# Seven-product feed-forward blocks: the remainder of the fourth weight slot moves from GpSimd to VectorE, and one corner is summed by matmuls onto a bank that ScalarE has filled

## The chip, the cores and the metric

The program runs on one core of a Trainium2 chip. The time is that of the device for one launch, in microseconds (us); lower is better.

## What is computed

The reference is an encoder of two layers on 512 tokens of width 1024, in float32. Each layer normalises its input, projects it, runs a latent attention and a state-space branch, mixes them, and then does a feed-forward (SwiGLU) block:

```
h   = x + W_o(...)
out = h + (silu(n @ w_gate) * (n @ w_up)) @ w_down      # n = RMSNorm(h)
```

`w_gate` and `w_up` are 1024 x 2816, `w_down` is 2816 x 1024. Only this block of the last layer (l = 1) is touched by the change.

## The kernel before, in words

Every float32 operand of a matmul is held as a high part (rounded to fp32r) and a low part (the remainder), and a product is three matmuls: high by high, high by low, low by high. ScalarE writes the high parts (`wh`), another engine subtracts them from the original to get the low parts (`wl`).

The last layer's gate and up projections are done by a scheme with seven products in place of eight. A step is one pair block q (0 to 21, even q is gate, odd q is up): two blocks of 128 output rows, by the two halves of the tokens (256 each), over the two halves of the inner dimension. Its weights come in two slabs of 512 KB (`pair_slab(q)` and the next). From them VectorE forms four sums (`sums_first`: two, `sums_last`: two). Four slots of `wh` and `wl` hold what the products read: slot 0 is the first slab as it is (P1 and P2), slot 1 the first two sums (P5, P6), slot 2 the last two (P3, P7), slot 3 one half of the second slab (P4). Each product is 12 matmuls of 256 columns.

The blocks come in three parts (`PARTS`): q = 0 to 7, 8 to 15 and 16 to 21. After each part its hidden rows go through the down projection (`down_steps`), whose weights use the same slots and stages.

TensorE's order in a block q is P2, P1, P5, P4 of block q-1 (called `corner`), P6, P3, P7. P6 adds onto P1's bank, P3 onto P5's, and P7 onto the bank of P6. PSUM banks: P2 in 2 + q%2, P1, P6, P7 and P4 in 4 + q%2, P5 and P3 in 6 + q%2.

The first corner of the output is P2 minus P1: ScalarE copies P1 to `part_sums` (`first_copied`), and VectorE subtracts it from P2 (`first_sum`, line 2065). The other three come from `corner` and `two`, `five` on ScalarE (copies) and from `other_sums` on VectorE (lines 2070 and 2073).

The loads have an order of their own. Four stages hold slabs, so pair q + 2 goes where pair q was. SyncE issues the loads in order, and for each it waits until the stage is free:

```
def freed_by_pair(q, i):
    sp.wait_ge(s34_ready, q + 1)
    sp.wait_ge(op_lo[0], q + 1)
    if i:
        sp.wait_ge(op_lo[3], q + 1)
```

`s34_ready` comes from `sums_last(q)`, `op_lo[0]` from VectorE's `low(0, q)`, `op_lo[3]` from the subtraction for slot 3, which in this kernel GpSimd does (line 724). On the other side `sums_first(q)` waits until both slabs of pair q have landed.

On each engine the work of the stage is a list in program order. ScalarE, in block q: `high(2, q)`, `first_copied(q)`, `high(0, q+1)`, `five(q)`, `corner(q-1)`, `high(3, q)`, `two(q)`, `high(1, q+1)`, `finished(q-1)`. VectorE: `other_sums(q-1)`, `low(2, q)`, `sums_first(q+1)`, `first_sum(q)`, `low(0, q+1)`, `sums_last(q+1)`, `scaled(q-1)`, `low(1, q+1)`, and in even blocks `rest(q-1)`.

Of the kernel before, what the change touches and what calls it, by code (L numbers as in the profile page):

```python
# [62 lines left out]
            "P7": (2, 1, X7), "P4": (3, 0, X4)}  # L63


def part_of(q):
    return next(h for h, (first, count) in enumerate(PARTS) if q < 2 * (first + count))

# [9 lines left out]
def pair_slab(q):  # L78
    return 2 * q + KT * part_of(q)
# [11 lines left out]
DONE = {}  # L91
for h in range(len(PARTS)):
    for q in range(first_of(h), last_of(h) + 1):
        for name in ("P2", "P1", "P5", "P4", "P6", "P3", "P7"):
            if name != "P4":
                DONE[q, name] = len(DONE) + 1
            elif q > first_of(h):
                DONE[q - 1, name] = len(DONE) + 1
    DONE[last_of(h), "P4"] = len(DONE) + 1
# [24 lines left out]
def build(nc, xT, stream, gcols, gqk, grows, dskip, params, cmat, rope, ident_in, out):  # L124
    with ExitStack() as ctx:
# [497 lines left out]
        def _(pool):  # L623
# [94 lines left out]
                for n in range(S_UP + 3, SLABS if l + 1 < DEPTH else S_FFN):  # L718
                    remainder(SLABS * l + n)

            for q in range(FB):
                s = fast_slot(3)
                pool.wait_ge(op_hi[3], q + 1)
                pool.tensor_tensor(wl[:, s, 0:QT], fast_stage(pair_slab(q) + 1)[:, QT:2 * QT],  # L724
                                   wh[:, s, 0:QT].bitcast(F32), ALU.subtract).then_inc(op_lo[3], 1)

        @block.scalar
        def _(act):
# [508 lines left out]
            def high(i, q):  # L1237
                if q == first_of(part_of(q)):
                    h = part_of(q)
                    if h:  # L1240
                        act.wait_ge(slab_done, RING + plain(h - 1, KT - RING + i) + 1)
                    else:
                        act.wait_ge(slab_done, RING + LAST - RING + i + 1)
                else:
                    act.wait_ge(prod_done, DONE[q - 1, ("P1", "P6", "P7", "P4")[i]])
                o = wh[:, fast_slot(i), :]
                if i == 0:
                    fast_loaded(pair_slab(q))
                    copy(o, fast_stage(pair_slab(q))).then_inc(op_hi[0], 1)
                elif i == 1:  # L1250
                    act.wait_ge(s12_ready, q + 1)
                    copy(o, wsum[:, 0:2, :].rearrange("p i c -> p (i c)")).then_inc(op_hi[1], 1)
                elif i == 2:
                    act.wait_ge(s34_ready, q + 1)
                    copy(o, wsum[:, 2:4, :].rearrange("p i c -> p (i c)")).then_inc(op_hi[2], 1)
                else:
                    fast_loaded(pair_slab(q) + 1)
                    copy(o[:, 0:QT], fast_stage(pair_slab(q) + 1)[:, QT:2 * QT]).then_inc(op_hi[3], 1)

            def down_high(h, m):  # L1260
                z, w = down_slab(h, m), 2 * PARTS[h][1] * P
                fast_loaded(z)
                if m < RING:
                    act.wait_ge(prod_done, DONE[last_of(h), ("P1", "P6", "P7", "P4")[m]])
                else:
                    act.wait_ge(slab_done, RING + plain(h, m - RING) + 1)
                copy(wh[:, fast_slot(m), 0:w], fast_stage(z)[:, 0:w]).then_inc(wh_ready, 1)
# [36 lines left out]
            def first_copied(q):  # L1304
                act.wait_ge(prod_done, DONE[q, "P1"])
                if q >= 2:
                    act.wait_ge(c11_done, q - 1)
                copy(part_sums[:, q % 2, 0, :], ps[:, 4 + q % 2, 0:HTOK]).then_inc(p_copied, 1)

            def five(q):  # L1310
                act.wait_ge(prod_done, DONE[q, "P5"])
# [25 lines left out]
            for h in range(len(PARTS)):  # L1337
                first, last = first_of(h), last_of(h)
                for q in range(first, last + 1):
                    high(2, q)  # L1340
                    first_copied(q)
                    if q < last:
                        high(0, q + 1)
                    else:
                        down_high(h, 0)
                    five(q)
                    if q > first:
                        corner(q - 1)
                    high(3, q)
                    two(q)  # L1350
                    if q == 0:
                        act.wait_ge(stat_ready, 2 * l + 2)
                        act.activation(rscol[:], ps[:, 0, 0:TT], ACT.Sqrt, bias=eps[:], scale=1.0 / D_MODEL).then_inc(rms_ready, 1)
                    if q == 1:
                        act.wait_ge(stat_ready, 2 * l + 3)
                        copy(RS[:], ps[:, 0, :]).then_inc(rms_ready, 1)
                    if q < last:
                        high(1, q + 1)
                    else:
                        down_high(h, 1)  # L1360
                    if q > first:
                        finished(q - 1)
                down_high(h, 2)
                corner(last)
                down_high(h, 3)
                finished(last)
                for m in range(KT):
                    if m < RING:
                        down_high(h, m + RING)
                    elif h + 1 < len(PARTS) and m < RING + 2:  # L1370
                        high(m - RING, last + 1)

        @block.vector
        def _(dve):
# [619 lines left out]
            def low(i, q):  # L1994
# [3 lines left out]
                dve.wait_ge(op_hi[i], q + 1)  # L1998
                tt(wl[:, s, :], source, wh[:, s, :].bitcast(F32), SUB).then_inc(op_lo[i], 1)  # L1999

            def down_low(h, m):
                s, w = fast_slot(m), 2 * PARTS[h][1] * P
                dve.wait_ge(wh_ready, plain(h, m) + 1 - RAW)
                tt(wl[:, s, 0:w], fast_stage(down_slab(h, m))[:, 0:w], wh[:, s, 0:w].bitcast(F32), SUB).then_inc(wl_ready, 1)
# [86 lines left out]
            for h in range(len(PARTS)):  # L2091
                first, last = first_of(h), last_of(h)
                for q in range(first, last + 1):
                    if q > first:
                        other_sums(q - 1)
                    low(2, q)
                    if q < last:
                        sums_first(q + 1)
                    first_sum(q)
                    if q < last:  # L2100
                        low(0, q + 1)
                        sums_last(q + 1)
                    else:
                        down_low(h, 0)
                    if q == 1:
                        dve.wait_ge(rms_ready, 2 * l + 3)
                    if q > first:
                        scaled(q - 1)
                    if q < last:
                        low(1, q + 1)  # L2110
                    else:
                        down_low(h, 1)
                    if q == 0:
                        dve.wait_ge(rms_ready, 2 * l + 2)
                        dve.reciprocal(rscol[:], rscol[:]).then_inc(rs_ready, 1)
                    if q > first and q % 2 == 0:
                        rest(q - 1)
# [25 lines left out]
        def _(pe):  # L2143
# [442 lines left out]
            def steps(q, name, ks):  # L2586
                i, half, o = PRODUCTS[name]
                bank = {"P2": 2, "P5": 6, "P3": 6}.get(name, 4) + q % 2
                s = fast_slot(i)
                for k in ks:  # L2590
                    if q == 0:
                        pe.wait_ge(xt_ready if o in (X4, X5, X6, X7) else xb_ready, k + 1)
                    at = slice(half * QT + k * P, half * QT + (k + 1) * P)
                    last = products(ps[:, bank, 0:HTOK], (wh[:, s, at], wl[:, s, at]), (XH[:, o, k, :], xl_of(o)[:, k, :]),
                                    k == 0 and name in ("P2", "P1", "P5"),
                                    k == 3, name not in ("P2", "P1", "P5"))
                return last

            def opening(q, name):
# [26 lines left out]
            for h in range(len(PARTS)):  # L2626
                first, last = first_of(h), last_of(h)
                count = 2 * PARTS[h][1]
                for q in range(first, last + 1):
                    if q == 0:  # L2630
                        for name in ("P1", "P5", "P2"):
                            if name == "P2":
                                pe.wait_ge(xm_ready, KT * l + 3 + KT)
                            opening(q, name)
                            steps(q, name, range(3))
                        for name in ("P2", "P1", "P5"):
                            steps(q, name, (3,)).then_inc(prod_done, 1)
                    else:
                        for name in ("P2", "P1", "P5"):
                            opening(q, name)  # L2640
                            steps(q, name, range(4)).then_inc(prod_done, 1)
                    if q == 1:
# [4 lines left out]
                    if q > first:  # L2647
                        corner(q - 1)
                    pe.wait_ge(p_copied, q + 1)
                    steps(q, "P6", range(4)).then_inc(prod_done, 1)  # L2650
                    if q == 0:
                        pe.wait_ge(x2_ready, KT * l + KT + 2)
# [115 lines left out]
```

## Time and profile before

| | |
|---|---|
| median of 3 runs | 1523.31 us (1523.0 to 1526.86) |
| the profiled execution, its own time | 1524.58 us |
| its span | 1522.4 us |
| TensorE busy | 1486.8 us, 98% |
| VectorE busy | 1099.5 us, 72% |
| ScalarE busy | 670.6 us, 44% |
| GpSimd busy | 462.0 us, 30% |
| stage of the change | from 1168 us to the end of the span |

The profile is one execution. PE is TensorE, PEld its weight loads, DVE is VectorE, ACT ScalarE, POOL GpSimd and SPq the queue of SyncE, which issues the loads. A row of a timeline gives start, duration, engine, line, operation, what is written and read, and in brackets the idle time before it and what ended that. L730 is a helper with which ScalarE does all its copies, L1999 is `low` for three slots, L2146 to L2148 are the three matmuls of a product.

### The profile page before, as it was taken

Reading aid. Unit: us, or ns where it says so; the run is one execution under the profiler, and the core shown is the slowest. Engines: PE = TensorE matmul, PEld = TensorE weight load, DVE = VectorE, ACT = ScalarE, POOL = GpSimd, SP = SyncE. Lnnn points to the kernel's source line nnn. Section 1 sums busy time; section 2 is a strip of 40 time slices with the busy share of each in tenths; the row PEclk is TensorE's granted clock in tenths of the full one; section 3 lists DMA queues with packets and bytes.
Section 4 is the critical chain, followed back from the end, with each engine's and each line's share of the span. In section 5 each row is a group of like instructions: output and inputs, shape, how many; then the busy total and the mean of one; then the engine's idle time right before and its main releaser. Section 6 shows DMA issues by size and latency. Waiting matters only on the chain.

```text
span 1522.4 us, 23041 instructions
## 1 busy us (share of the span) xinstructions
PE 1486.8 (98%) x8954; PEld 1221.0 (80%) x8954; DVE 1099.5 (72%) x1469; ACT 670.6 (44%) x1146; POOL 462.0 (30%) x254
## 2 busy tenths in 40 slices
PE   8999998999999999999999999999999999999998
PEld 3555897878878878887888888887787998998997
DVE  5999888768448997568432782586888995896794
ACT  4563258852452222232332413587435652453361
POOL 0000053544444454443544323444542120110010
PEclk9999999999999999999999999999999999999999
DMA  6568720142333244443437642102331333234223
GB/s 248 163 195 294 296 84 1 43 124 83 97 113 97 77 167 158 145 140 112 163 106 276 214 153 89 56 1 70 111 103 65 111 97 126 84 99 137 70 92 116
DMA packets 73499, 189.51 MB, mean 124 GB/s; under 512 B 23600, under 2 KB 32176, under 8 KB 69296
## 3 DMA queue, kind: packets, MB, share of 16 engines
q1 hardware_dynamic: 41952, 145.18, 28.3%
q10 hardware_dynamic: 31440, 42.87, 8.7%
q8 instruction: 71, 1.16, 0.3%
q14 instruction: 36, 0.29, 0.1%
HBM read 155.52 MB, written 32.51 MB: 124 GB/s over the span
## 4 chain that ended last, share of the span: by engine, by line
PE 67%; DVE 17%; DVEq 5%; ACT 4%; issue 3%; DMA 1%; POOLq 1%; POOL 1%; SPq 0%; ACTq 0%
PE ps L2146 20%; PE ps L2148 20%; PE ps L2147 20%; PE ps L2295 2%; DVE wl L1999 2%; DVE work L1382 1%; ACT prob L1148 1%; PE ps L2201 1%; PE ps L2272 1%; DVEq L1562 1%; DVEq L1509 1%; PE ps L2240 1%; DVE wsum L1990 1%; PE ps L2286 1%; PE ps L2459 1%
## 5 line engine op out<-in xcount | busy, mean ns | idle before, releaser
L632 POOL TENSOR_TENSOR wl<-stage,wh 128x1024 fp32r<-128x1024 f32 x138 | 356.7, 2591 | 645.2 <-ACT wh L730 456.2
L730 ACT ACTIVATE wh<-stage 128x1024 fp32r<-128x1024 f32 (+2 forms) x178 | 181.0, 1023 | 221.9 <-PE ps L2148 103.4
L2146 PE MATMUL ps<-XH,wh 128*128 128x256 f32 x616 | 174.8, 284 | 3.7 <-DVE wl L1999 2.8
L2148 PE MATMUL ps<-XH,wl 128*128 128x256 f32 x616 | 173.8, 282 | 0.0
L2147 PE MATMUL ps<-XLr,wh 128*128 128x256 f32 x528 | 148.5, 281 | 0.0
L2146 PE MATMUL ps<-xg2h,wh 128*128 128x512 f32 x352 | 140.3, 399 | 0.0
L2148 PE MATMUL ps<-xg2h,wl 128*128 128x512 f32 x352 | 139.2, 396 | 0.0
L2147 PE MATMUL ps<-xg2l,wh 128*128 128x512 f32 x352 | 139.2, 396 | 0.0
L2146 PEld LDWEIGHTS ps<-XH,wh 128*128 128x128 f32 x616 | 116.8, 190 | 5.2 <-DVE wl L1999 3.2
L2148 PEld LDWEIGHTS ps<-XH,wl 128*128 128x128 f32 x616 | 116.8, 190 | 0.0
L2201 PE MATMUL ps<-X,slabs 128*128 128x512 f32 x224 | 100.7, 604 | 7.2 <-DMA X<-in_xT 5.8
L2147 PEld LDWEIGHTS ps<-XLr,wh 128*128 128x128 f32 x528 | 99.8, 189 | 0.2
L2201 PEld LDWEIGHTS ps<-X,slabs 128*128 128x128 f32 x224 | 42.2, 193 | 58.9 <-issue 46.5
L2146 PE MATMUL ps<-xgh,wh 128*128 128x512 f32 x208 | 84.4, 406 | 0.0
L2148 PE MATMUL ps<-xgh,wl 128*128 128x512 f32 x208 | 82.3, 396 | 0.0
L2147 PE MATMUL ps<-xgl,wh 128*128 128x512 f32 x208 | 82.3, 396 | 0.0
L2146 PEld LDWEIGHTS ps<-xg2h,wh 128*128 128x128 f32 x352 | 66.1, 188 | 16.3 <-issue 0.6
L2148 PEld LDWEIGHTS ps<-xg2h,wl 128*128 128x128 f32 x352 | 66.1, 188 | 16.0
L2147 PEld LDWEIGHTS ps<-xg2l,wh 128*128 128x128 f32 x352 | 66.2, 188 | 15.9 <-issue 0.2
L724 POOL TENSOR_TENSOR wl<-stage_more,wh 128x512 fp32r<-128x512 f32 x11 | 17.8, 1616 | 198.7 <-ACT wh L730 198.7
L2146 PE MATMUL ps<-hidh,wh 128*128 128x512 f32 x176 | 70.2, 399 | 3.2 <-DVE X L1968 1.7
L2146 PE MATMUL ps<-hid1h,wh 128*128 128x512 f32 x176 | 69.7, 396 | 0.0
(346 smaller groups left out, 3748.0 us busy)
## 6 DMA issues: line engine op xcount, KB each, us to landing
stage<-in_stream SPq DMA_DIRECT2D x178, 512.0 KB, 3.4
stage_more<-in_stream SPq DMA_DIRECT2D x34, 512.0 KB, 3.8
CPTR<-ctd_scr ACTq DMA_DIRECT2D x6, 1664.0 KB, 8.2
slabs<-in_stream SPq DMA_DIRECT2D x17, 512.0 KB, 5.5
InT<-in_scr ACTq DMA_DIRECT2D x6, 1024.0 KB, 6.1
ctd_scr<-CPp SPq DMA_DIRECT2D x4, 1152.0 KB, 7.8
ctd_scr<-CPp ACTq DMA_DIRECT2D x4, 1152.0 KB, 6.6
in_scr<-BPI SPq DMA_DIRECT2D x4, 1024.0 KB, 5.0
```

The source lines that it names most:

```text
L632: pool.tensor_tensor(wl[:, s, :], stage[:, (n - RAW) % STAGES, :], wh[:, s, :].bitcast(F32), ALU.subtract).then_inc(wl_ready, 1)
L724: pool.tensor_tensor(wl[:, s, 0:QT], fast_stage(pair_slab(q) + 1)[:, QT:2 * QT], wh[:, s, 0:QT].bitcast(F32), ALU.subtract).then_inc(op_lo ...
L730: return act.activation(o, i, ACT.Copy, **kw)
L1148: act.activation(prob[e][:], ps[:, a % 2, :], ACT.Exp, bias=nmx[:, e:e + 1], accum_out=psm[:, hp % 2, u:u + 1]).then_inc(exp_ready, 1)
L1382: tt(t[0], a[1], b[1], MUL)
L1509: dve.drain()
L1999: tt(wl[:, s, :], source, wh[:, s, :].bitcast(F32), SUB).then_inc(op_lo[i], 1)
L2146: pe.matmul(o, wt[0], x[0], start=start, stop=False, skip_group_check=onto)
L2147: pe.matmul(o, wt[0], x[1], start=False, stop=False, skip_group_check=onto)
L2148: return pe.matmul(o, wt[1], x[0], start=False, stop=stop, skip_group_check=onto)
L2201: return pe.matmul(o, raw_slab(n)[:, k * P:(k + 1) * P], X[:, k, :], start=start, stop=stop)
L2295: last = pe.matmul(ps[:, 6 + gi, q * NCH:(q + 1) * NCH], CP[h, r, 2 * q + d, at:at + P], S[h, r, 2 * q + d, :], start=False, stop=(d == 1 ...
```

## The change

For all blocks but 0, P2 moves behind P4, and TensorE's order becomes P1, P5, P4 of q-1, P2, P6, P3, P7. `first_copied` writes minus P1 into P2's bank instead of `part_sums`, P2's matmuls add onto it, and a new copy on ScalarE, `first_corner`, takes the finished corner out. VectorE's `first_sum` stays for block 0 only. Slot 0 is now free when P2 is done (`freeing`), and ScalarE makes `high(0, q+1)` after `five`, `corner` and `first_corner`. The subtraction for slot 3 leaves GpSimd and becomes VectorE's `corner_low(q)`, which stands after `low(1, q+1)`; `low(0, q+1)` moves behind `scaled(q-1)`.

```diff
+def freeing(q, i):
+    return (("P1" if q == 0 else "P2"), "P6", "P7", "P4")[i]
...
-        for name in ("P2", "P1", "P5", "P4", "P6", "P3", "P7"):
+        for name in ("P2", "P1", "P5", "P4", "P6", "P3", "P7") if q == 0 else ("P1", "P5", "P4", "P2", "P6", "P3", "P7"):
...
-            for q in range(FB):
-                s = fast_slot(3)
-                pool.wait_ge(op_hi[3], q + 1)
-                pool.tensor_tensor(wl[:, s, 0:QT], fast_stage(pair_slab(q) + 1)[:, QT:2 * QT],
-                                   wh[:, s, 0:QT].bitcast(F32), ALU.subtract).then_inc(op_lo[3], 1)
...
-                    act.wait_ge(prod_done, DONE[q - 1, ("P1", "P6", "P7", "P4")[i]])
+                    act.wait_ge(prod_done, DONE[q - 1, freeing(q - 1, i)])
...
-                copy(part_sums[:, q % 2, 0, :], ps[:, 4 + q % 2, 0:HTOK]).then_inc(p_copied, 1)
+                if q == 0:
+                    copy(part_sums[:, q % 2, 0, :], ps[:, 4 + q % 2, 0:HTOK]).then_inc(p_copied, 1)
+                else:
+                    copy(ps[:, 2 + q % 2, 0:HTOK], ps[:, 4 + q % 2, 0:HTOK], scale=-1.0).then_inc(p_copied, 1)
+
+            def first_corner(q):
+                i = q // 2
+                act.wait_ge(prod_done, DONE[q, "P2"])
+                if i >= 2:
+                    act.wait_ge(hidl_ready, FB * l + i - 1)
+                copy((act_, up)[q % 2][:, i % 2, 0, 0:HTOK], ps[:, 2 + q % 2, 0:HTOK]).then_inc(c11_done, 1)
...
                     first_copied(q)
+                    five(q)
+                    if q > first:
+                        corner(q - 1)
+                    if not (q == 0):
+                        first_corner(q)
                     if q < last:
                         high(0, q + 1)
                     else:
                         down_high(h, 0)
-                    five(q)
-                    if q > first:
-                        corner(q - 1)
                     high(3, q)
...
+            def corner_low(q):
+                s = fast_slot(3)
+                dve.wait_ge(op_hi[3], q + 1)
+                tt(wl[:, s, 0:QT], fast_stage(pair_slab(q) + 1)[:, QT:2 * QT], wh[:, s, 0:QT].bitcast(F32), SUB)\
+                    .then_inc(op_lo[3], 1)
...
-                    first_sum(q)
+                    if q == 0:
+                        first_sum(q)
                     if q < last:
-                        low(0, q + 1)
                         sums_last(q + 1)
-                    else:
-                        down_low(h, 0)
...
                     if q < last:
+                        low(0, q + 1)
                         low(1, q + 1)
                     else:
+                        down_low(h, 0)
                         down_low(h, 1)
+                    corner_low(q)
...
-                        for name in ("P2", "P1", "P5"):
+                        for name in ("P1", "P5"):
                             opening(q, name)
                             steps(q, name, range(4)).then_inc(prod_done, 1)
...
                     pe.wait_ge(p_copied, q + 1)
+                    if not (q == 0):
+                        opening(q, "P2")
+                        steps(q, "P2", range(4)).then_inc(prod_done, 1)
                     steps(q, "P6", range(4)).then_inc(prod_done, 1)
```

## Rows read from the trace of the kernel before

**Rows 1.** One block: length, busy PE, PEld, DVE, ACT, POOL; clock, DMA

```profile
1195.60:1205.50 9.90, 9.90 (x86) 9.90 (x85) 9.57 (x12) 5.93 (x10) 1.68 (x1) 1.00 0.31 106
```

**Rows 2.** Timeline of TensorE: first matmuls of P6 and P3 of block 3

```profile
1208.01 0.28 PE L2146 MATMUL ps<-XH,wh 128*128 128x256 f32 x1
...
1209.43 0.28 PE L2146 MATMUL ps<-XH,wh 128*128 128x256 f32 x1
```

**Rows 3.** Timeline of TensorE around one of its stops

```profile
1226.45 0.28 PE L2148 MATMUL ps<-XH,wl 128*128 128x256 f32 x1
1227.02 0.35 PE L2146 MATMUL ps<-XH,wh 128*128 128x256 f32 x1 [0.29 <-DVE act L2073]
```

**Rows 4.** VectorE: a line's shortest, median, longest (ns), then its timeline

```profile
L1990 DVE TENSOR_TENSOR wsum<-stage x11: 677/687/1791, 1180.8 to 1469.6; 128x512 f32<-128x512 f32 x11
...
1190.72 1.23 DVE L2080 TENSOR_TENSOR act<-act,RS 128x1024 f32<-128x1024 f32 x1 [1.08 <-ACT RS L730]
...
1215.83 1.23 DVE L1999 TENSOR_TENSOR wl<-wsum,wh 128x1024 fp32r<-128x1024 f32 x1 [0.28 <-ACT wh L730]
1217.15 0.69 DVE L1984 TENSOR_TENSOR wsum<-stage 128x512 f32<-128x512 f32 x1
1217.92 0.69 DVE L1986 TENSOR_TENSOR wsum<-wsum,stage 128x512 f32<-128x512 f32 x1
1218.52 0.42 DVE L2065 TENSOR_TENSOR act<-ps,part_sums 128x256 f32<-128x256 f32 x1
1218.86 1.22 DVE L1999 TENSOR_TENSOR wl<-stage,wh 128x1024 fp32r<-128x1024 f32 x1
1219.99 1.78 DVE L1990 TENSOR_TENSOR wsum<-stage 128x512 f32<-128x512 f32 x1
```

**Rows 5.** Timeline of GpSimd, block 3

```profile
1209.19 1.93 POOL L724 TENSOR_TENSOR wl<-stage,wh 128x512 fp32r<-128x512 f32 x1 [8.26 <-ACT wh L730]
```

**Rows 6.** Timeline of ScalarE

```profile
1180.35 1.06 ACT L730 ACTIVATE wh<-wsum 128x1024 fp32r<-128x1024 f32 x1
...
1209.63 0.39 ACT L730 ACTIVATE part_sums<-ps 128x256 f32<-128x256 f32 x1 [0.51 <-PE ps L2148]
1209.91 1.05 ACT L730 ACTIVATE wh<-wsum 128x1024 fp32r<-128x1024 f32 x1
```

**Rows 7.** Loads: an issue, times to landing (all; the issue at 666.31), a consumer

```profile
1211.21 0.33 SPq L587 DMA_DIRECT2D stage<-in_stream  x1
...
DMA to landing us min/median/max: 3.1/3.8/5.4
...
stage<-in_stream SPq DMA_DIRECT2D x1, 512.0 KB, 3.3
...
669.66 1.06 ACT L730 ACTIVATE wh<-stage 128x1024 fp32r<-128x1024 f32 x1 [1.18 <-DMA stage<-in_stream]
```

**Rows 8.** Timeline of TensorE: first products of parts, first matmuls of down projections

```profile
1253.86 0.40 PE L2146 MATMUL ps<-hid1h,wh 128*128 128x512 f32 x1
...
1300.09 0.28 PE L2146 MATMUL ps<-XH,wh 128*128 128x256 f32 x1
...
1378.59 0.39 PE L2146 MATMUL ps<-hid1h,wh 128*128 128x512 f32 x1
...
1424.80 0.28 PE L2146 MATMUL ps<-XH,wh 128*128 128x256 f32 x1
...
1483.03 0.39 PE L2146 MATMUL ps<-hid1h,wh 128*128 128x512 f32 x1
```

**Rows 9.** TensorE after two stops: timeline, then windows (columns as rows 1)

```profile
565.12 0.50 PE L2146 MATMUL ps<-hidh,wh 128*128 128x512 f32 x1 [1.70 <-DVE X L1968]
...
1171.67 0.38 PE L2146 MATMUL ps<-XH,wh 128*128 128x256 f32 x1 [2.56 <-DVE wl L1999]
...
565.00:569.00 4.00, 3.88 (x17) 3.17 (x18) 4.00 (x3) 0.48 (x1) 3.03 (x1) 1.00 0.16 66
1172.00:1176.00 4.00, 4.00 (x23) 4.00 (x22) 3.47 (x8) 2.53 (x3) 0.00 (x0) 0.57 0.00 0
```

More of the change, by code:

```diff
@@ L1263, in down_high @@
                 if m < RING:
-                    act.wait_ge(prod_done, DONE[last_of(h), ("P1", "P6", "P7", "P4")[m]])
+                    act.wait_ge(prod_done, DONE[last_of(h), freeing(last_of(h), m)])
                 else:
@@ L2594, in steps @@
                     last = products(ps[:, bank, 0:HTOK], (wh[:, s, at], wl[:, s, at]), (XH[:, o, k, :], xl_of(o)[:, k, :]),
-                                    k == 0 and name in ("P2", "P1", "P5"),
-                                    k == 3, name not in ("P2", "P1", "P5"))
+                                    k == 0 and (name in ("P1", "P5") or name == "P2" and q == 0),
+                                    k == 3, not (name in ("P1", "P5") or name == "P2" and q == 0))
                 return last
```

## The prediction

> **What bounds the kernel now.** I read the page first, whose busy times stand in the table above: TensorE in 98% of the span, VectorE in 72%. The change touches only the last layer's feed-forward, so I cut that out. A window over one block shows TensorE busy for the whole 9.90 us, VectorE for 9.57 of them, ScalarE for 5.93 and GpSimd for 1.68 [rows 1]. So TensorE sets the time of a block and VectorE is a third of a microsecond behind it: nearly full, too.
>
> One product is 12 matmuls, 0.118 us apart, and the next product starts 1.42 us after it [rows 2]. Seven make a block of 9.94 us. Where does TensorE stop? Going through all its matmuls of this stage, I find five stops by VectorE in the blocks, three of them as in [rows 3]: the last sum of block 4 (line 2073) ends at 1226.87, TensorE starts 0.15 us later, 0.57 us after its last matmul instead of 0.12, and its first matmul takes 0.35 instead of 0.28, which is 0.07 more. All five together cost about 2.2 us. That is all that a less loaded VectorE can give back.
>
> **The removed and the added work.** Half of VectorE's list of one block stands in [rows 4], and I use the distances between starts: 1.14 us for 1024 columns (1218.86 to 1219.99), 0.60 for 512, 0.33 for 256, and 0.17 more where a drain follows. Removed from it is `first_sum` (0.33), for all blocks but 0. Added is `corner_low`, 512 columns of subtraction, for which I take 0.60 (0.69 to its end, as lines 1984 and 1986). GpSimd's subtraction disappears. While it runs, VectorE's own instruction is held: line 1990 takes 0.68 us at the least and 1.78 in block 4 [rows 4], while GpSimd's own row takes 1.93 [rows 5]. That gives back about 1.1 us. VectorE thus has 1.1 + 0.33 - 0.60 = 0.8 us less to do in a block, if nothing holds it.
>
> ScalarE keeps its list and gets one copy more of 256 columns (0.28 between starts [rows 6]), so some 6.2 us of 9.94. `first_copied` now writes PSUM with a scale. No row shows that. From below I put it at nothing over today's 0.38. From above, it starts 1.62 us into a block and P2 needs it at 4.26, so up to 2.2 us more are hidden by P5 and P4. I take 0.38. P2 on a filled bank is the same 12 matmuls: 0.
>
> **What moves, and what waits for it.** The remainder of slot 3 frees the second half of a stage, and SyncE waits for it (`freed_by_pair`, i = 1) before it loads the second slab of the pair after the next. Today GpSimd ends at 1209.19 + 1.93 = 1211.12 and SyncE issues at 1211.21 [rows 5, 7], 8.9 us into a block that began four products before 1208.01, at 1202.33 [rows 2]. A slab lands 3.8 us later in the median of all 68 [rows 7], so at 1215.0. `sums_first` of the next iteration starts at 1217.15 [rows 4]: 2.1 us to spare.
>
> After the change `corner_low(q)` stands behind `low(1, q+1)`, which needs ScalarE's `high(1, q+1)`, which needs P6. With t from a block's P1: P2 is done at 5.68, ScalarE starts 0.20 after that (1209.63 against 1209.43 [rows 2, 6]), so `first_corner` 5.88, `high(0)` 6.16, `high(3)` 7.11, `two` 7.63, `high(1)` 7.91 to 8.97 (the distance of two starts is the duration less 0.1, so 0.28 for 256 columns, 0.95 for 1024 [rows 6] and about 0.52 between them for 512). VectorE: `low(1)` 9.00, `corner_low` 10.14 to 10.83. The next `sums_first` would want to start at 12.5 in the one kind of block and 13.9 in the other. The slab, issued at 10.92, lands at about 14.7.
>
> So `sums_first` waits for the DMA, and this is no single wait but a ring, because everything behind it moves the next `corner_low`. One turn of it: to SyncE 0.09; transfer 3.8; landing to consumer 0.05 (666.31 + 3.3 against ScalarE's 669.66 [rows 7]); drain 0.09; then VectorE 0.77 + 0.60 (`sums_first`), 0.77 + 0.77 (`sums_last`, 512 columns and a drain each, with GpSimd out of the way), 1.14 `scaled`, 1.14 `low(0)`, 1.14 `low(1)`, 0.69 `corner_low` = 7.02. Together 11.05 us against TensorE's 9.94: 1.11 us a turn. `rest`, `other_sums` and `low(2)` (3.0 us) fit inside the transfer.
>
> The transfer is the uncertain term: 3.1 at the least, 3.8 in the median, 5.4 at the most [rows 7]. In the ring SyncE finds the next slab's conditions long met and issues it 0.4 us later. The nine transfers of today that have another 0.4 to 0.5 us behind them all lie around that median, so I take 3.8, and keep both ends.
>
> The Trainium skill (DMA: Bandwidth & Descriptors, its section on the fixed cost) fits 2.0 us plus bytes over 436 thousand per us for another kind of issue, which is 3.2 us for 512 KB. By that the ring would be an estimated 10.4 us and the loss 9 instead of 17 us. The shortest transfers here agree with it, the median of 3.8 does not.
>
> **The sum.** E is the end of `corner_low`. In a part's first block (no P4) the same list gives E = 9.41. Each further block but the last adds a turn. P4 of the last block but one waits for `rest` and `other_sums`: E - 0.08 + 1.14 + 0.33 + 0.41 + 0.15 = E + 1.95. Five products and the 0.07 later (7.17) `down_steps` start.
> Part 1: 9.41 + 6 x 11.05 + 1.95 + 7.17 = 84.83, today 1378.59 - 1300.09 = 78.50 [rows 8]: +6.3.
> Part 2: 9.41 + 4 x 11.05 + 9.12 = 62.73, today 1483.03 - 1424.80 = 58.23: +4.5.
> Part 0: `high(1, 1)` ends at 1181.41 [rows 6], so E = 1181.44 + 1.14 + 0.69 = 1183.27. The first turn is held by the copy of RS (line 2080 at 1190.72 [rows 4]) and ends at 1190.72 + 3.42 + 0.69 = 1194.83; five more turns give 1250.08, plus 9.12 = 1259.2, today 1253.86: +5.3.
> In parts 0 and 1 the last P4 then needs `other_sums`, which now come after `corner_low`: 10.74, 11.07 to 11.48, plus 0.15, against 9.94 + 1.41: 0.28 and the 0.07, twice, 0.7. Part 2's shorter down slabs hide it. In the other even blocks the same chain with `rest` ends at 12.78, where P4 is due at 12.78: nothing to spare, and nothing lost.
> The five stops of today are inside these differences. Sum: 6.3 + 4.5 + 5.3 + 0.7 = 16.8 us. The profiled execution took 1524.58 (span 1522.4 and 2.2 around it), giving 1541.4; the median 1523.31 gives 1540.1. I say 1540.
>
> **Rivals.**
> 1. *The transfer is hidden and the relief wins.* For it speaks that VectorE is 97% busy in a block, that GpSimd's hold of 1.1 us a block goes away, and that the five stops have VectorE as their cause. The Trainium skill (SBUF — State Buffer, on the shared port pair) says that of a VectorE instruction with two SBUF inputs and a GpSimd one the later is fully blocked; by it the whole overlap returns, which leads here. In rows: -2.2 + 0.7 and up to 0.15 at 8 even blocks, so 1522 to 1523, not slower. The point from which it decides is the length of the transfer: 9.94 - 7.02 - 0.23 = 2.7 us; the shortest is 3.1. Chance 0.10.
> 2. *The second transfer slows the first.* The longest took 5.4: 16 turns x 1.6 more, 1566; half as bad, 1553. Against it: in today's closely spaced pairs the first lands at about the median. Chance 0.08.
> 3. *The clock falls.* TensorE now stops about 1.1 us in each block. After the stop of 2.56 us before 1171.67 the granted clock was 0.57 over the next 4 us; after one of 1.70 us it stayed at 1.00 [rows 9]. Those 4 us held 23 matmuls, which at full clock take 23 x 0.118 = 2.7, so 1.3 us were lost. If the short stops did that too, a block would take 9.94 + 1.3 = 11.24, 0.2 more than the ring: 16 turns add 3 us, 1543, more if two stops of a block each do it. Chance 0.06.
> The ring itself, with a transfer of 3.1 to 4.4, has 0.76.
>
> **How the numbers follow.** What can be told from no change is 0.3%, 4.6 us. Only rival 1 is within it, 0.11 with a remainder; a gain over 4.6 us would need more than the 2.2 us there are, 0.03; slower 0.86. The range goes by the transfer: 3.1 gives 16 x 0.7 = 11 less, 1529; a mean of 4.4 gives 1550. That leaves out rival 1 and the worse half of rival 2.
>
> **What would show it.** In the changed profile `sums_first` (its first instruction) should be idle about 1 to 2 us before it in every block but a part's first, ended by the stage's DMA, and SyncE should issue the odd slab right behind the slot 3 subtraction. The same instruction should start every 11.0 us; line 1990 should be at 0.68 throughout. TensorE should wait before P1 for `low(0)`, and in even blocks before P4 for `other_sums`. GpSimd should have no row in the stage. I am wrong if `sums_first` starts every 9.9 us, or if the wait sits before P2 (the fill) or P7 (`two`, which I give 0.4 us to spare).

## The result

The changed kernel takes 1541.12 us (median of 4 runs, 1540.46 to 1543.79), the kernel before 1524.46 (4 runs, 1523.0 to 1526.86). The ratio is 1.0111, with a 95% interval of 1.0092 to 1.013. Forecast were 1540 us and a range of 1529 to 1550. The three runs of the table ahead had 1523.31 as their median; with the fourth it is 1524.46.

The profiled execution of the changed kernel took 1541.02 us, its span is 1539.2. Its page answers to the table of before: TensorE is busy a little more, VectorE 14 us less, and GpSimd 36 us less.

```profile
span 1539.2 us, 23039 instructions
PE 1492.0 (97%) x8954; PEld 1221.1 (79%) x8954; DVE 1085.8 (71%) x1470; ACT 677.4 (44%) x1167; POOL 425.9 (28%) x232
```

The timeline of VectorE over one turn of the ring, its list of block 10, which prepares block 11 (L1995 is the first instruction of `sums_first`, L2001 and L2003 `sums_last`, L2100 `scaled`, L2010 the `low`s, L2015 `corner_low`, L2105 `rest`, L2087 and L2090 `other_sums`):

```profile
1329.78 0.69 DVE L1995 TENSOR_TENSOR wsum<-stage 128x512 f32<-128x512 f32 x1 [2.24 <-DMA stage<-in_stream]
1330.55 0.69 DVE L1997 TENSOR_TENSOR wsum<-wsum,stage 128x512 f32<-128x512 f32 x1
1331.16 0.69 DVE L2001 TENSOR_TENSOR wsum<-stage 128x512 f32<-128x512 f32 x1
1331.92 0.69 DVE L2003 TENSOR_TENSOR wsum<-wsum,stage 128x512 f32<-128x512 f32 x1
1332.71 1.23 DVE L2100 TENSOR_TENSOR up<-up,act 128x1024 f32<-128x1024 f32 x1
1333.85 1.22 DVE L2010 TENSOR_TENSOR wl<-stage,wh 128x1024 fp32r<-128x1024 f32 x1
1334.98 1.22 DVE L2010 TENSOR_TENSOR wl<-wsum,wh 128x1024 fp32r<-128x1024 f32 x1
1336.12 0.69 DVE L2015 TENSOR_TENSOR wl<-stage_more,wh 128x512 fp32r<-128x512 f32 x1
1336.72 1.22 DVE L2105 TENSOR_TENSOR hid1l<-up,hid1h 128x1024 fp32r<-128x1024 f32 x1
1337.86 0.41 DVE L2087 TENSOR_TENSOR act<-part_sums,ps 128x256 f32<-128x256 f32 x1
...
1340.95 0.69 DVE L1995 TENSOR_TENSOR wsum<-stage_more 128x512 f32<-128x512 f32 x1 [1.21 <-DMA stage_more<-in_stream]
```

From the first to the last row are 11.17 us. VectorE runs without a gap from the sums to the end of `corner_low` at 1336.81. SyncE's queue follows, and behind it the first of its two loads with its time to landing, and all loads of the line:

```profile
1336.89 0.33 SPq L591 DMA_DIRECT2D stage_more<-in_stream  x1
1337.31 0.38 SPq L591 DMA_DIRECT2D stage<-in_stream  x1
```

```profile
stage_more<-in_stream SPq DMA_DIRECT2D x1, 512.0 KB, 3.9
...
DMA to landing us min/median/max: 3.1/3.9/6.0
```

0.08 us after `corner_low` the odd slab is asked for, and the next one 0.42 behind it. It lands at 1340.8, and VectorE starts again at 1340.95. In [rows 5, 7] the same request came 8.9 us into a block and nobody waited for it; here both kinds of block wait, 2.2 us in the one and 1.2 in the other (up to 2.5 in a part's first turn), 16 times in all. The list of VectorE's waits gives the total, the number and the longest:

```profile
DVE wsum L1995 <- DMA stage<-in_stream: 17.8, 8, 2.3
...
DVE wsum L1995 <- DMA stage_more<-in_stream: 12.9, 8, 2.5
```

What TensorE makes of it (the last matmul before P1 of block 11 and its first, then the same for the P4 behind it, which is that of block 10):

```profile
1333.98 0.28 PE L2166 MATMUL ps<-XH,wl 128*128 128x256 f32 x1
1335.12 0.39 PE L2164 MATMUL ps<-XH,wh 128*128 128x256 f32 x1 [0.87 <-DVE wl L2010]
...
1337.95 0.28 PE L2166 MATMUL ps<-XH,wl 128*128 128x256 f32 x1
1338.75 0.36 PE L2164 MATMUL ps<-XH,wh 128*128 128x256 f32 x1 [0.52 <-DVE act L2090]
```

The starts that answer to [rows 8] are:

```profile
1258.47 0.39 PE L2164 MATMUL ps<-hid1h,wh 128*128 128x512 f32 x1
...
1305.05 0.28 PE L2164 MATMUL ps<-XH,wh 128*128 128x256 f32 x1
...
1390.34 0.39 PE L2164 MATMUL ps<-hid1h,wh 128*128 128x512 f32 x1
...
1436.91 0.28 PE L2164 MATMUL ps<-XH,wh 128*128 128x256 f32 x1
...
1499.87 0.39 PE L2164 MATMUL ps<-hid1h,wh 128*128 128x512 f32 x1
```

Part 1 takes 1390.34 - 1305.05 = 85.29 us in place of 78.50, part 2 62.96 in place of 58.23.

**A finer measure.** Runs of one kernel spread over some 6 us, in one case over 10. Much of that lies ahead of the change: the stage's first product started between 1165.6 and 1171.9 us in the eleven profiles of this study. So beside each ratio I give the stage: the time in the profiled execution from the start of its first product to the start of its last matmul. Before it is 350.15 us, changed 367.97, 17.8 longer. The stage is not free of noise either: after TensorE's stop of 2.56 us [rows 9] some of the matmuls behind it start every 0.21 us in place of 0.12. By the timelines it is 13 to 16 of them, which makes an estimated 0.3 us between kernels.

### The profile page after: what moved, and what is told of

Read it like the earlier page. It is cut to its first block, busy times and chain, and to the rows that moved or that the text cites. A ratio compares the mean times of both kernels' runs of the same rounds, so it can differ in the third digit from the quotient of the medians.

```text
span 1539.2 us, 23039 instructions
## 1 busy us (share of the span) xinstructions
PE 1492.0 (97%) x8954; PEld 1221.1 (79%) x8954; DVE 1085.8 (71%) x1470; ACT 677.4 (44%) x1167; POOL 425.9 (28%) x232
## 4 chain that ended last, share of the span: by engine, by line
PE 62%; DVE 19%; DVEq 5%; DMA 4%; ACT 4%; issue 4%; POOLq 1%; POOL 1%; SPq 0%; ACTq 0%
PE ps L2164 18%; PE ps L2166 18%; PE ps L2165 18%; DMA stage<-in_stream 2%; DMA stage_more<-in_stream 2%; PE ps L2313 2%; DVE wl L2010 2%; DVE work L1393 1%; ACT prob L1147 1%; PE ps L2219 1%; PE ps L2290 1%; DVEq L1573 1%; DVE wl L2015 1%; DVEq L1520 1%; PE ps L2258 1%
## 5 line engine op out<-in xcount | busy, mean ns | idle before, releaser
L2166 PE MATMUL ps<-hid1h,wl 128*128 128x512 f32 x176 | 69.6, 396 | 0.0
```

Of the source, the lines that this page charges most:

```text
L2166: return pe.matmul(o, wt[1], x[0], start=False, stop=stop, skip_group_check=onto)
```

## The experiments

The theory is the ring: late remainder, load, `sums_first`, and so on to the next remainder. Rival A is that the reordered P2 and the fill by ScalarE cost the time, rival B that VectorE has too much to do.

| kernel | stage, us | turn, us | median, us | ratio to before (95%) |
|---|---|---|---|---|
| before | 350.15 | 10.31 | 1524.46 | |
| changed | 367.97 | 11.10 | 1541.12 | 1.0111 (1.0092 to 1.013) |
| slot 3 on GpSimd again | 354.14 | 10.16 | 1527.9 | 1.0022 (1.0009 to 1.0035) |
| odd slab in halves | 355.31 | 10.22 | 1531.05 | 1.0039 (1.0025 to 1.0053) |
| one place up | 349.87 | 10.03 | 1526.56 | 1.0009 (0.9998 to 1.0021) |
| corner_low alone | 366.88 | 11.41 | 1540.18 | 1.0103 (1.0081 to 1.0125) |
| extra work in the ring | 380.27 | 11.67 | 1556.96 | 1.021 (1.0189 to 1.023) |
| extra work outside | 370.66 | 11.01 | 1546.97 | 1.015 (1.0135 to 1.0165) |
| early version | 348.99 | 9.94 | 1522.71 | 0.9991 (0.9979 to 1.0004) |
| early, and low(0, 2) first | 348.24 | 9.94 | 1522.13 | 0.9984 (0.9974 to 0.9995) |
| early, on the kernel before | 347.77 | 9.95 | 1521.28 | 0.9989 (0.9976 to 1.0003) |

Each ratio is against runs of the kernel before that were made beside it (for the experiments their medians are 1524.51, 1524.68 and 1523.67). The last kernel and its partner ran on another chip than the other experiments. The turn is the mean of five distances in part 1, from the start of `sums_first(10)` to that of `sums_first(15)`. Where nothing holds VectorE it is TensorE's 9.94. In the kernel before it is 10.31: there VectorE, held by GpSimd, falls behind and TensorE has not yet had to wait for it by the end of the five.

### The slot 3 remainder back on GpSimd

```diff
+            for q in range(FB):
+                s = fast_slot(3)
+                pool.wait_ge(op_hi[3], q + 1)
+                pool.tensor_tensor(wl[:, s, 0:QT], fast_stage(pair_slab(q) + 1)[:, QT:2 * QT],
+                                   wh[:, s, 0:QT].bitcast(F32), ALU.subtract).then_inc(op_lo[3], 1)
...
-                    corner_low(q)
```

> The changed kernel with one thing undone: the slot 3 remainder is subtracted by GpSimd again. Ring theory (late remainder, then load, then sums_first): GpSimd starts when high(3) ends, 7.7 us into a block, ends near 9.5, and no VectorE instruction stands between the sums and it, so the ring is open: sums_first still waits up to 1 us for the load, but starts every 9.94 us. 1525 us, 1523 to 1528. Rival A (the reordered P2 and the fill by ScalarE cost the time): both are kept, so 1541. Rival B (VectorE is short of time): VectorE loses 0.60 us and gets back GpSimd's hold of 1.1 us, so 1541 or more.

It took 1527.9 us and its stage 354.14. Of the 17.8 us 13.8 are gone, with P2's new place, the fill and `first_corner` kept, so rival A has room for the other 4 us at most (the early versions below keep all three as well and leave it none). The 4 us are of another kind, as VectorE's and GpSimd's timelines show:

```profile
1358.47 2.32 DVE L2015 TENSOR_TENSOR wl<-stage_more,wh 128x1024 fp32r<-128x1024 f32 x1
```

```profile
1358.07 1.65 POOL L728 TENSOR_TENSOR wl<-stage,wh 128x512 fp32r<-128x512 f32 x1 [8.12 <-ACT wh L734]
```

GpSimd still holds a VectorE instruction, and now it is `low(0)`: 2.32 us in place of 1.22, for which P1 waits. GpSimd's row ends at 1359.72; 1.22 us later is 1360.94, and `low(0)` ends at 1360.79, so nearly all of its 1.22 us lie behind GpSimd's instruction. The expectation's sum had no term for this hold and was 3 us too low, at the upper end of its range.

### The odd slab in two halves

Only SyncE's loads and the counts of those who wait for them change. The half that `corner_low` reads waits for it, the other half does not.

```diff
             def fast_slab(z):
-                sp.dma_start(fast_stage(z), stream[LAST + z]).then_inc(fast_staged[z % 4], 16)
+                for c in range(1 + z % 2):
+                    part = slice(c * QT, (c + 1) * QT) if z % 2 else slice(0, 2 * QT)
+                    sp.dma_start(fast_stage(z)[:, part], stream[LAST + z][:, part]).then_inc(fast_staged[z % 4], 16)
+                    yield
...
-                if i:
-                    sp.wait_ge(op_lo[3], q + 1)
...
                             freed_by_pair(q, i)
-                            fast_slab(z)
+                            for c, _ in enumerate(fast_slab(z)):
+                                if i and c == 0:
+                                    sp.wait_ge(op_lo[3], q + 1)
```

> The changed kernel with VectorE, ScalarE and TensorE as they are; only SyncE loads the odd slab of each two in two halves, and only the half that corner_low reads waits for it. Ring theory: what stands in the ring is a load of 256 KB, about 2.4 us in place of 3.85, so a turn takes 9.7 us, under the 9.94 of TensorE: 1524 us, 1522 to 1528. Rivals A (fill and order of P2) and B (VectorE short of time): nothing of theirs is touched, 1541.

The stage fell from 367.97 to 355.31 us without a touch on any compute engine's list: 12.7 of the 17.8 us. The size of a load sets the size of the loss, so the load is in the ring. The median of 1531.05 us lies above the expected range all the same, and that is a miss in the size of the term: the 2.4 us had no row behind them, and the half loads that a sum waited for took 2.7 to 3.4 us, 3.0 in the mean, where whole ones had taken 3.8. VectorE's rows (L2018 `corner_low`, L1998 `sums_first`), then the load between them, of 3.2 us, and all loads of the line:

```profile
1339.17 0.68 DVE L2018 TENSOR_TENSOR wl<-stage,wh 128x512 fp32r<-128x512 f32 x1
...
1343.29 0.69 DVE L1998 TENSOR_TENSOR wsum<-stage 128x512 f32<-128x512 f32 x1 [1.63 <-DMA stage<-in_stream]
```

```profile
stage<-in_stream SPq DMA_DIRECT2D x1, 256.0 KB, 3.2
...
DMA to landing us min/median/max: 2.7/3.8/6.0
```

With 3.0 us in it the ring is 10.3 us; the turns of part 1 took 10.22 in the mean, still above 9.94. The Trainium skill (DMA: Bandwidth & Descriptors, on the fixed cost, given for another kind of issue) would give an estimated 2.6 us for 256 KB; the shortest loads in the ring, 2.7, are near it, the longest, 3.4, are not; all of them had a full slab's load some 0.4 us behind.

### corner_low one place up

```diff
                     if q < last:
                         low(0, q + 1)
+                    else:
+                        down_low(h, 0)
+                    corner_low(q)
+                    if q < last:
                         low(1, q + 1)
                     else:
-                        down_low(h, 0)
                         down_low(h, 1)
-                    corner_low(q)
```

> The changed kernel with corner_low(q) one place earlier on VectorE, between low(0, q+1) and low(1, q+1); ScalarE and TensorE as in the change. Ring theory: the ring loses low(1), 1.14 us of the 11.13 that a turn took, and comes to 9.99, TensorE's 9.94; the last P4 of a part no longer waits: 1523 us, 1522 to 1526. If VectorE's load or the fill by ScalarE were the cause: 1541.

The stage came to 349.87 us and the turn to 10.03, against 9.99 expected; two lines of VectorE's list changed places and all of the loss is gone. The median of 1526.56 is 3 us above what was expected and just outside the range, with an interval that includes no change. In the profiled execution, of 1527.87 us, the stage began at 1171.86, 4 us later than in the kernel before, and all that comes ahead of it is the same program.

### corner_low alone, on the kernel before

GpSimd's loop is removed, and `corner_low(q)` stands behind `low(1, q+1)`; TensorE's and ScalarE's lists are those of before, and `first_sum` stays.

```diff
                         down_low(h, 1)
+                    corner_low(q)
```

> The kernel before with one part of the change alone: slot 3's remainder on VectorE behind low(1); P2, first_sum and ScalarE's list as before. Ring theory: the ring is longer by first_sum, 11.4 us a turn, but P4 stands one product later behind it: part 1 +6.5, part 2 +4, part 0 +5.5, 1540 us, 1535 to 1545. Rival A (fill and order of P2): they are absent, 1523.

1540.18 us, the stage 366.88: this one move makes 16.7 of the 17.8 us. The five turns in part 1 took 11.36 to 11.45 us, as the longer ring of 11.4 asks.

### Extra work in the ring and outside

One addition of 512 columns on a scratch tile, ahead of `corner_low` (shown) or behind it; nothing is left out.

```diff
                 dve.wait_ge(op_hi[3], q + 1)
+                tt(sq1[:, 0, :], sq1[:, 1, :], sq1[:, 1, :], ADD)
                 tt(wl[:, s, 0:QT], fast_stage(pair_slab(q) + 1)[:, QT:2 * QT], wh[:, s, 0:QT].bitcast(F32), SUB)\
                     .then_inc(op_lo[3], 1)
```

> The changed kernel with one more VectorE addition of 512 columns (0.60 us between starts) of a scratch tile in front of corner_low, in the ring. It leaves nothing of the computation out. Ring theory: a turn of 11.73 us, 16 turns x 0.60 = 9.6, and 0.6 at the last P4 of two parts: 1552 us, 1549 to 1556.

> The same extra addition right behind corner_low, outside the ring, where VectorE waits 1.0 to 2.3 us for the load anyway. Ring theory: a turn stays 11.13; only P4 of the last block but one and the last P4 of a part come 0.6 later, 3 x 0.6 + 2 x 0.6 = 3: 1544 us, 1542 to 1546. If VectorE's total work were what counts, the same as with the addition in front, 1552.

Against the changed kernel the stage grew by 12.3 us with the addition in the ring and by 2.7 with the same addition outside. VectorE's rows of the two, around the same place (`sq<-sq` is the addition):

```profile
1353.51 0.69 DVE L2015 TENSOR_TENSOR sq<-sq 128x512 f32<-128x512 f32 x1
1358.95 0.69 DVE L1995 TENSOR_TENSOR wsum<-stage 128x512 f32<-128x512 f32 x1 [2.36 <-DMA stage<-in_stream]
1365.29 0.68 DVE L2015 TENSOR_TENSOR sq<-sq 128x512 f32<-128x512 f32 x1
1370.74 0.69 DVE L1995 TENSOR_TENSOR wsum<-stage_more 128x512 f32<-128x512 f32 x1 [1.23 <-DMA stage_more<-in_stream]
```

```profile
1351.94 0.68 DVE L2017 TENSOR_TENSOR sq<-sq 128x512 f32<-128x512 f32 x1
1356.05 0.69 DVE L1995 TENSOR_TENSOR wsum<-stage 128x512 f32<-128x512 f32 x1 [1.63 <-DMA stage<-in_stream]
1362.98 0.69 DVE L2017 TENSOR_TENSOR sq<-sq 128x512 f32<-128x512 f32 x1
1367.04 0.69 DVE L1995 TENSOR_TENSOR wsum<-stage_more 128x512 f32<-128x512 f32 x1 [0.43 <-DMA stage_more<-in_stream]
```

Inside, the waits stay at 2.4 and 1.2 us and the turn shown is 11.8; outside, the waits shrink by the 0.6 to 0.8 that the addition fills and the turn stays at 11.0. So it isn't how much VectorE does that counts but where it does it. Inside, I had left out one term: the first `corner_low` of each part comes 0.6 later too. The three parts took 3.6, 3.9 and 2.8 us more, the two stretches between them 0.6 each. The last down projection took 0.7 more, for which no sum had a term. Outside, the 2.7 us are made up otherwise than expected as well: 0.8, 0.2 and 0.2 in the parts, 0.6 in each stretch between them and 0.3 in the last down projection. Both medians miss their ranges, by 1 us at the upper end; they lie 5 and 3 us above what was expected, of which the stages have 1.5 and none.

### The early versions

`high(3, q)` right behind `corner(q-1)`, `corner_low(q)` between `sums_last` and `scaled`; the second version has besides, in block 1 alone, `low(0, 2)` ahead of the wait for the copy of RS (the lines with `low(0, q + 1)` are in the second alone).

```diff
                     if q > first:
                         corner(q - 1)
+                    high(3, q)
                     if not (q == 0):
                         first_corner(q)
...
-                    high(3, q)
                     two(q)
...
                         sums_last(q + 1)
+                    corner_low(q)
                     if q == 1:
+                        low(0, q + 1)
                         dve.wait_ge(rms_ready, 2 * l + 3)
...
                     if q < last:
-                        low(0, q + 1)
+                        if q != 1:
+                            low(0, q + 1)
...
-                    corner_low(q)
```

> The changed kernel with the slot 3 work earlier: high(3, q) right behind corner(q-1) on ScalarE, corner_low(q) between sums_last and scaled on VectorE. Ring theory: behind the sums only 0.6 us is left in the ring, a turn of 7.6 us, no wait for the load; the five stops of the kernel before go as well, since GpSimd no longer holds VectorE. 1522 us, 1521 to 1524, so 0.1 to 0.2% under the kernel before. Rival A: 1541. Rival B: the same VectorE work, 1541.

> The early version (high(3) behind corner, corner_low behind sums_last) and besides, in block 1 alone, low(0, 2) ahead of the wait for the copy of RS, which held it in the early version and stopped TensorE for 0.87 us before P1 of block 2. 0.8 us less than the early version: about 1522 us, ratio to the kernel before 0.9985, between 0.998 and 0.999 where the five stops of 2.2 us are gone as well.

The stages are 348.99 and 348.24 us, 1.2 and 1.9 less than before. By the sum of the expectation a turn could now be 7.6 us, so TensorE's 9.94 rules, and its windows in part 1 of the first version (columns as rows 1) are full:

```profile
1320.00:1330.00 10.00, 10.00 (x87) 10.00 (x86) 9.55 (x13) 6.37 (x11) 0.00 (x0) 1.00 0.32 106
1330.00:1340.00 10.00, 10.00 (x87) 10.00 (x86) 9.09 (x12) 6.41 (x11) 0.00 (x0) 1.00 0.35 107
```

The second has a ratio of 0.9984 (0.9974 to 0.9995), so it is faster than the kernel before, and than the changed one; the first, at 0.9991, can't be told from no change.

### The early place on the kernel before

GpSimd's loop is removed here, too.

```diff
                     if q < last:
                         low(0, q + 1)
                         sums_last(q + 1)
                     else:
                         down_low(h, 0)
+                    corner_low(q)
                     if q == 1:
```

> The kernel before with one line moved from GpSimd to VectorE: slot 3's remainder as corner_low(q) between sums_last and scaled. P2, first_sum and ScalarE's list stay as they were before. high(3) is ready 6.8 us into a block and VectorE comes to corner_low at about 7.0, so the odd slab is asked for at 7.7, earlier than GpSimd allowed (8.9). If the gain of the early versions is the end of GpSimd's hold on VectorE, this kernel has all of it: the stage 1.9 us shorter than before, 348.3 us, 1522.5 us in all, ratio about 0.9985. If the reordered P2 and the fill by ScalarE give part of the gain, it lies between 348.3 and 350.2.

The stage is 347.77 us, the shortest of all, with P2 in its old place and neither the fill nor `first_corner`. Part 1 takes 78.11, 78.11 and 78.09 us in the three early kernels and 78.50 before, part 2 58.23 in all four; the rest of the gain is in part 0. So the reordered P2 gives nothing beside it, nor does it cost anything. What is left as the cause of the gain is the end of GpSimd's hold: the odd slab is also asked for earlier here, but in the kernel before no sum waited for a load. Of the 2.4 us some 0.2 are the matmuls at the lower clock, 13 here and 15 before. The ratio, 0.9989 (0.9976 to 1.0003), can't be told from no change, nor from that of the version above.

## Why the prediction was right

**The ring.** Forecast: 11.05 us a turn. `corner_low` started at 1313.77 and 1380.53 in blocks 8 and 14, six turns of 11.13. From SyncE's issue to VectorE's start these six took 3.92 to 4.18 us, 4.02 in the mean, against 3.8 + 0.05 + 0.09 = 3.94, and that is the whole difference. Most of it is the transfer (4.0 in the first, 3.8 to 3.9 in the others); the landing in the turn shown is 0.15 us ahead of VectorE's start, against 0.14. Each of the distances on VectorE (0.77, 0.61, 0.76, 0.79, 1.14, 1.13, 1.14) is that of the rows of before to within 0.02.

**The sum.** Part 0 was forecast at +5.3 and came to +5.6 (1258.47 - 1166.91 against 1253.86 - 1167.88), part 1 +6.3 and +6.8, part 2 +4.5 and +4.7, the last P4 of parts 0 and 1 together 0.7 and 0.7. In all 16.8 and 17.8. In parts 1 and 2 the missing 0.7 is ten turns that were forecast 0.06 to 0.08 too short. In part 0 the five turns after the wait for RS took 11.04 each, and the missing 0.3 lies ahead of them: `corner_low(1)` ended 27.25 us after the part's start, against 26.95. The medians differ by 16.7 us, nearer to the 16.8 than the stage is; with runs that spread over 3 to 4 us that closeness is luck. One statement of the sum was wrong without harm: P4 of the other even blocks was to lose nothing, and TensorE stopped 0.52 us before five of them. The next P1 waits for `low(0)` in any case, so the turn is no longer for it.

**The relief.** Forecast were five stops of 2.2 us gone. It is there, but only to be seen where the ring is broken: 1.9 us in the early version with `low(0, 2)` first, 2.4 on the kernel before, and in the changed kernel line 2001 takes 0.68 or 0.69 us throughout. GpSimd's hold itself was put at 1.1 us a block. In the kernel before it falls on 20 VectorE instructions of the stage, of several lines, and lengthens them by 0.3 to 1.1 us, 18.6 in all. By the two pages of the profile VectorE was busy for 13.7 us less, which is 0.6 a block and not 0.8. The Trainium skill (SBUF — State Buffer, on the shared port pair) says that of a VectorE instruction with two SBUF inputs and a GpSimd one that reads SBUF the later is fully blocked. The held `low(0)` of the kernel with GpSimd, 2.32 in place of 1.22, agrees.

**The fill.** Bounded by nothing and 2.2 us, taken as 0.38. The copy from PSUM to PSUM took 0.37 in all 21 rows, and TensorE never waited for it:

```profile
L729 ACT ACTIVATE ps<-ps x21: 368/368/368, 1182.6 to 1490.8; 128x256 f32<-128x256 f32 x21
```

**The rivals.** That the transfer is hidden needed one within 2.7 us; the shortest was 3.1. That the second transfer slows the first is true, but by less than the rival had it, and the forecast had the effect in its 3.8 us already. In the kernel before, nine pairs of loads in the blocks stand 1.25 us apart or more, and their first took 3.2 to 3.5 us; ten (the prediction counts nine) stand 0.4 to 0.5 us apart, and their first took 3.5 to 4.1. An issue of each kind, at 1231.15 and at 1441.65:

```profile
stage<-in_stream SPq DMA_DIRECT2D x1, 512.0 KB, 3.2
...
stage<-in_stream SPq DMA_DIRECT2D x1, 512.0 KB, 4.1
```

In the changed kernel's ring all are of the second kind, 3.6 to 4.0 us. The early kernels say the same for part 1, up to 1365 us: the first of two took 3.4 to 3.6 us where the next is 1.1 us or more behind (the version with `low(0, 2)` first), and 3.8 to 4.2 where it is 0.42 behind (the one on the kernel before). No run changed this distance alone. The clock did not fall. Over 84 us of part 1, which hold eight stops of 0.20 to 0.93 us, the granted clock was 1.00, the upper of its two levels (columns as rows 1):

```profile
1306.00:1390.00 84.00, 79.12 (x652) 77.37 (x651) 67.30 (x84) 47.27 (x77) 0.00 (x0) 1.00 0.28 89
```

## What to carry to other kernels

When a step that frees a buffer moves, follow the buffer round: the free, the queue that reloads it, the transfer, the first consumer, and every instruction in program order from there to the next free. If that ring is longer than the block of the engine that sets the time, the difference is paid in every block, however idle the engines look; here VectorE was busy for 0.6 us less in a block and the kernel lost 1.1 in every turn of the ring. And put the step that frees the buffer ahead of all that doesn't free one: two lines exchanged took the whole loss away.

## What the runs showed of the hardware

I had not expected that half a slab would take 2.7 to 3.4 us to land, 3.0 in the mean, when a whole one takes 3.6 to 4.0 in the same place, 3.8 in the mean: half the bytes saved 0.8 us of 3.8 in the load and 0.9 in the mean turn. Nor that a load takes longer for another issued behind it: 3.2 to 3.5 us with the next one 1.25 us or more away, 3.5 to 4.1 with one 0.4 to 0.5 us behind. And the clock did not mind short stops, as I had thought likely: TensorE stopped for 0.20 to 0.93 us 22 times in the stage of the changed kernel after its first stop of 2.56 us, and in the windows over parts 0, 1 and 2 (1176 to 1258, 1306 to 1390, 1437 to 1499) the granted clock was 1.00.
